# Leaving out 27 idle TensorE products in the norm between the first MLP and the gating unit

## The chip, the cores and the metric

The kernel runs on one core of a Trainium2 chip. A core has TensorE (PE, with its weight loads shown apart as PEld), VectorE (DVE), ScalarE (ACT), GpSimd (POOL) and the sync engine (SP), which issues DMAs. The engines run at the same time and wait for each other through semaphores. The metric is the device time of one execution in microseconds, and lower is better.

## The reference

Two transformer blocks run one after the other on 512 tokens of 1024 channels, in float32. The first block has two layers (a pooling mixer, then a spatial gating unit, "sgu"), each followed by an MLP of width 4096. The second block has attention, a recurrent mixer and a gated feed-forward. The place of the change is the norm that opens the second layer, right behind the first MLP:

```python
for i in range(DEPTH):
    mod = c_act @ ada_w[i] + ada_b[i]
    sh1, sc1, g1, sh2, sc2, g2 = jnp.split(mod, 6, axis=-1)
    h = modulate(rmsnorm(x, norm_mix_g[i]), sh1, sc1)      # i == 1: this norm
    y = pool_mixer(h, ...) if i == 0 else sgu_mixer(h, sgu_w_in, ...)
    x = x + g1[:, None, :] * y
    h = modulate(rmsnorm(x, norm_mlp_g[i]), sh2, sc2)
    x = x + g2[:, None, :] * sq_relu_mlp(h, mlp_w1[i], mlp_w2[i])

def rmsnorm(x, g):
    y = x * lax.rsqrt(jnp.mean(x * x, axis=-1, keepdims=True) + RMS_EPS)
    return y * g
def sgu_mixer(h, w_in, ...):
    z = gelu(h @ w_in)      # the first use of this norm's h
```

## The kernel before

Activations lie transposed: `xT[:, k]` holds 128 channels (k = 0 to 7) by 512 tokens. Weights come in slabs of 512 by 512 through DMAs that SP issues. ACT rounds each slab into its high part (`w_hi`, line 1665) and DVE subtracts to get its low part (`w_lo`, line 2309), in a ring of two slabs. TensorE then makes three products for one (high by high, high by low, low by high), each 128 rows by 512 columns, 48 for a slab; that is the function `slab`, line 762. The activations are split in the same way into `h_hi` and `h_lo`.

Each engine has one program, written out by hand in the order in which it runs, and semaphores alone tie the engines together. There is no scheduler: what stands behind a waiting instruction on an engine waits too.

The norm `NORM_MIX1` goes through these steps. The last slab of `mlp(0, ...)` fills four banks. DVE adds each to `xT` (line 2667) and ACT squares it (line 1683). DVE sums the squares (line 2336). `norm_mean` lets TensorE sum over the channels with 16 products of one column each (line 733, each recorded twice). ACT takes the root (line 1687), DVE the reciprocal (line 2324) and puts it on a diagonal (line 2326). `norm_spread` is one product of 512 columns, recorded as two (line 837), that spreads the diagonal over all partitions in a bank. Then, for k = 0 to 7, DVE scales `xT[:, k]` into `tmp` (line 2346), ACT makes `h_hi[:, k]` (line 1693) and DVE makes `h_lo[:, k]` (line 2356). The first slab of `sgu_in` (`two_slabs("sgu_in", 0, ...)`, with `k_outer=True`) begins as soon as k = 0 is made and does 12 products for each k.

The function `keep_busy(s, times, b=6)` multiplies a slab's `w_hi` with itself `times` times into bank 6 (line 820). Nobody reads what it makes, and the next true use of the bank starts it anew. It stands three times in this norm: 7 products ahead of the mean, 6 between the mean and the spread, and 14 behind the spread. It is used at two later places as well (lines 1236 and 1619), which the change leaves alone.

Three other places of the program come up in the prediction. The norm ahead of the first MLP (`NORM_MLP0`, some 60 to 76 us into the trace) has the same steps with no such products. The gating unit's last heads and its output slab (lines 1044 and 1098, 528 to 537 us) run just behind this part. The norm ahead of the second MLP (596 to 600 us) uses `mlp1_by_halves` and DVE line 2784.

Of the kernel before, what the change touches and what calls it, by code (L numbers as in the profile page):

```python
# [92 lines left out]
SLABS = {"mlp0": 0, "sgu_in": 41, "sgu_out": 49, "mlp1": 53, "proj": 94, "w_out": 104, "ffn": 108}  # L93
# [632 lines left out]
def tensor_program(te, t, m, sem):  # L726
# [88 lines left out]
    def keep_busy(s, times, b=6):  # L815

        w_hi = m.ring(s)[0]
        te.wait_ge(sem("hi_made"), s + 1)
        for _ in range(times):
            te.matmul(bank[:, b], w_hi[:, 0, 0:P], w_hi[:, 0], start=True, stop=True)  # L820

    def norm_mean(norm, squares):

        name, count = added(norm, additions(norm))
        te.wait_ge(sem(name), count)
        apart = norm in LAST_APART
        for j in range(4):
            mm = in_halves(bank[:, 4, j:j + 1], squares[:, 3, P * j:P * j + P], m.mean_ones[:, 0:1], j == 0, not apart)
        if apart:
            te.wait_ge(sem("squared"), 8 * norm + 8)  # L830
            for j in range(4):
                mm = in_halves(bank[:, 4, j:j + 1], squares[:, 0, P * j:P * j + P], m.mean_ones[:, 0:1], False, True)
        mm.then_inc(sem("meaned"), 1)

    def norm_spread(norm):
        te.wait_ge(sem("diag_made"), norm + 1)
        te.matmul(m.rstd_bank, ones[:, :], m.rstd_diag[:, :, :].rearrange("p j t -> p (j t)"),
                  start=True, stop=True).then_inc(sem("spread"), 1)
# [210 lines left out]
    norm_spread(NORM_MLP0)  # L1049
    ada_sums(7)  # L1050
    mlp(0, NORM_MLP0)
    keep_busy(SLABS["sgu_in"], 7)
    norm_mean(NORM_MIX1, m.quartered["mlp0"].squares)
    keep_busy(SLABS["sgu_in"], 6)
    norm_spread(NORM_MIX1)
    keep_busy(SLABS["sgu_in"], 14)


    def two_slabs(name, g, hi, lo, before_k=None, weights_stationary=True, k_outer=False, beside=None):
# [2531 lines left out]
def program(nc, t, out):  # L3591
    m, sem = Places(nc), Sems(nc)
    tensor_program(nc.tensor, t, m, sem)
    scalar_program(nc.scalar, t, m, sem)
    vector_program(nc.vector, t, m, sem)
    gpsimd_program(nc.gpsimd, t, m, sem)
    sync_program(nc.sync, t, out, m, sem)
# [47 lines left out]
```

## Time and profile before

| | us |
|---|---|
| median of 3 runs | 1757.35 (1757.21 to 1757.66) |
| the profiled execution, its own time | 1758.68 |
| its span, first to last instruction | 1757.3 |
| TensorE busy | 1715.4 (98%) |
| DVE busy | 1227.5 (70%) |
| ACT busy | 757.1 (43%) |

Between the span and the profiled execution's own time lie 1.4 us, and that execution took 1.3 us more than the median of the runs. Matmuls are pipelined: a product of 512 columns is shown with some 0.39 us, while the next one starts 0.227 us after it, so the distance between starts is what a product costs in a stream. The granted clock is given as a share: 1.00 is 2.4 GHz and 0.50 is 1.2 GHz.

### The profile page before, as it was taken

To read this page: it belongs to the slowest core of one execution; us is meant where nothing else is said; L and a number is where in the kernel's file an instruction comes from. 1 tells how busy PE (TensorE), PEld (TensorE's weight loads), DVE (VectorE), ACT (ScalarE), POOL (GpSimd) and SP (SyncE) were. 2 spreads that over 40 slices of the span, in tenths; PEclk is the share of its full clock that TensorE was granted. 3 is DMA by queue.
4 is the path that set the end of the run, shared out by engine and by line. 5 is a ranking of instruction groups with operands and counts; after the bars stand their busy time and mean duration, and the time that the engine had idled before them with its cause. 6 is when DMAs were issued, how large, how long until landed. Compare 5 with 4: busy or idle time off the path is not lost. (4 is left out here: it accounts for less than half of the span.)

```text
span 1757.3 us, 23082 instructions
## 1 busy us (share of the span) xinstructions
PE 1715.4 (98%) x9391; PEld 1397.5 (80%) x9391; DVE 1227.5 (70%) x1435; ACT 757.1 (43%) x933; POOL 126.0 (7%) x131
## 2 busy tenths in 40 slices
PE   7899999999999999999999998999999999999997
PEld 4488888888789888888887786778888888888886
DVE  4588797876874675747457777775768579578579
ACT  4354435333332553535345523453544344344344
POOL 0111010000100000000000011110000000000002
PEclk9899999999999999999999999999999999999999
DMA  9967484745632445445221331003344435336324
GB/s 369 409 195 229 129 252 134 260 143 192 216 105 87 145 120 144 144 120 168 96 67 65 103 86 51 5 1 121 120 120 123 141 96 154 126 80 189 99 72 132
DMA packets 141673, 246.45 MB, mean 140 GB/s; under 512 B 15117, under 2 KB 50597, under 8 KB 141312
## 3 DMA queue, kind: packets, MB, share of 16 engines
q1 hardware_dynamic: 122432, 192.76, 32.3%
q0 software_dynamic: 18992, 51.62, 11.9%
q8 instruction: 75, 1.23, 0.3%
q10 hardware_dynamic: 144, 0.59, 0.1%
q14 instruction: 30, 0.25, 0.0%
HBM read 239.69 MB, written 6.83 MB: 140 GB/s over the span
## 5 line engine op out<-in xcount | busy, mean ns | idle before, releaser
L2309 DVE TENSOR_TENSOR w_lo<-raw,w_hi 128x2048 fp32r<-128x2048 f32 x99 | 227.5, 2298 | 160.7 <-ACT w_hi L1665 160.2
L1665 ACT ACTIVATE w_hi<-raw 128x2048 fp32r<-128x2048 f32 x103 | 197.2, 1915 | 275.3 <-PE bank L762 170.4
L762 PE MATMUL bank<-h_hi,w_hi 128*128 128x512 f32 x720 | 285.1, 396 | 6.1 <-DVE h_lo L2356 2.9
L762 PE MATMUL bank<-h_hi,w_lo 128*128 128x512 f32 x720 | 281.0, 390 | 0.0
L762 PE MATMUL bank<-h_lo,w_hi 128*128 128x512 f32 x720 | 280.9, 390 | 0.0
L762 PE MATMUL bank<-f_lo,w_hi 128*128 128x512 f32 x496 | 193.0, 389 | 0.0
L762 PE MATMUL bank<-f_hi,w_hi 128*128 128x512 f32 x496 | 193.0, 389 | 0.0
L762 PE MATMUL bank<-f_hi,w_lo 128*128 128x512 f32 x496 | 193.0, 389 | 0.0
L762 PEld LDWEIGHTS bank<-h_hi,w_hi 128*128 128x128 f32 x720 | 135.6, 188 | 38.0 <-issue 10.5
L762 PEld LDWEIGHTS bank<-h_hi,w_lo 128*128 128x128 f32 x720 | 135.4, 188 | 28.6
L762 PEld LDWEIGHTS bank<-h_lo,w_hi 128*128 128x128 f32 x720 | 135.6, 188 | 27.6 <-issue 0.5
L787 PE MATMUL bank<-w_hi,blocks_hi_mlp 128*128 128x512 f32 x336 | 131.2, 391 | 0.0
L787 PE MATMUL bank<-w_hi,blocks_lo_mlp 128*128 128x512 f32 x336 | 130.8, 389 | 0.0
L787 PE MATMUL bank<-w_lo,blocks_hi_mlp 128*128 128x512 f32 x336 | 130.8, 389 | 0.0
L762 PEld LDWEIGHTS bank<-f_hi,w_lo 128*128 128x128 f32 x496 | 93.1, 188 | 19.5
L762 PEld LDWEIGHTS bank<-f_lo,w_hi 128*128 128x128 f32 x496 | 93.1, 188 | 19.3
L762 PEld LDWEIGHTS bank<-f_hi,w_hi 128*128 128x128 f32 x496 | 93.1, 188 | 19.1
L2309 DVE TENSOR_TENSOR w_lo<-raw_more_ffn,w_hi 128x2048 fp32r<-128x2048 f32 x30 | 68.7, 2290 | 46.7 <-ACT w_hi L1665 46.5
L1665 ACT ACTIVATE w_hi<-raw_more_ffn 128x2048 fp32r<-128x2048 f32 x30 | 57.5, 1916 | 77.8 <-PE bank L787 37.2
L787 PE MATMUL bank<-w_hi,blocks_hi_ffn 128*128 128x512 f32 x224 | 87.3, 390 | 0.6 <-issue 0.6
L787 PE MATMUL bank<-w_hi,blocks_lo_ffn 128*128 128x512 f32 x224 | 87.2, 389 | 0.0
L787 PE MATMUL bank<-w_lo,blocks_hi_ffn 128*128 128x512 f32 x224 | 87.2, 389 | 0.0
(486 smaller groups left out, 3138.2 us busy)
## 6 DMA issues: line engine op xcount, KB each, us to landing
raw<-in_mlp_w SPq DMA_DIRECT2D x82, 512.0 KB, 5.1
ada_ring<-in_ada_w SPq DMA_DIRECT2D x12, 2048.0 KB, 15.1
ada_ring<-in_ada_w POOLq DMA_DIRECT2D x16, 1024.0 KB, 7.3
raw_more_mlp<-in_mlp_w SPq DMA_DIRECT2D x32, 512.0 KB, 4.8
raw<-in_w_ffn_up SPq DMA_DIRECT2D x32, 512.0 KB, 5.0
raw_more_ffn<-in_w_ffn_up SPq DMA_DIRECT2D x32, 512.0 KB, 4.9
xT<-in_mlp_w SPq DMA_DIRECT2D x26, 512.0 KB, 4.8
raw<-in_w_in SPq DMA_DIRECT2D x20, 512.0 KB, 4.5
```

Source lines behind the costliest of these rows:

```text
L762: mm = te.matmul(bank[:, b + n], x, y, start=first and k == 0 and j == 0, stop=last and k == 3 and j == 2, skip_group_check=s in (SLABS["m ...
L787: mm = te.matmul(bank[:, b + n], x, w[:, k], start=start and k == 0 and j == 0, stop=k == 3 and j == 2, skip_group_check=True)
L1665: se.activation(m.ring(s)[0], m.raw_place(s), ACT.Copy).then_inc(sem("hi_made"), 1)
L2309: ve.tensor_tensor(lo, m.raw_place(s), hi.bitcast(F32), ALU.subtract).then_inc(sem("lo_made"), 1)
```

## The change

Three calls are taken out of TensorE's program, 7 + 6 + 14 = 27 products. Nothing else is edited.

```diff
     mlp(0, NORM_MLP0)
-    keep_busy(SLABS["sgu_in"], 7)
     norm_mean(NORM_MIX1, m.quartered["mlp0"].squares)
-    keep_busy(SLABS["sgu_in"], 6)
     norm_spread(NORM_MIX1)
-    keep_busy(SLABS["sgu_in"], 14)
```

Each call also had a wait on `hi_made` for the first slab of `sgu_in`; that slab's own products wait for the same count. On TensorE the stretch between the last slab of the first MLP and the first products on `sgu_in` then reads as follows, as a difference of the two programs.

```order
 L762 MATMUL bank<-blocks_lo_mlp,w_hi 128x512
 L762 MATMUL bank<-blocks_hi_mlp,w_lo 128x512
-L820 MATMUL bank<-w_hi 128x512 x7
 L733 MATMUL bank<-mean_ones,quarter_u_mlp 64x1 x16
-L820 MATMUL bank<-w_hi 128x512 x6
 L837 MATMUL bank<-rstd_diag,ones 128x512
-L820 MATMUL bank<-w_hi 128x512 x14
 L762 MATMUL bank<-w_hi,h_hi 128x512
 L762 MATMUL bank<-w_lo,h_hi 128x512
```

No instruction has moved past another. ACT, DVE, POOL and SP keep their instructions and their order.

## Rows read from the trace of the kernel before

**Rows 1.** The page: span, busy time by engine

```profile
span 1757.3 us, 23082 instructions
PE 1715.4 (98%) x9391; PEld 1397.5 (80%) x9391; DVE 1227.5 (70%) x1435; ACT 757.1 (43%) x933; POOL 126.0 (7%) x131
```

**Rows 2.** Waits of TensorE behind 433 us: total, times, longest

```profile
PE bank L762 <- DVE h_lo L2784: 2.9, 1, 2.9
PE bank L1468 <- DVE pt L3173: 2.8, 7, 0.8
```

**Rows 3.** Timeline of the norm, TensorE: start, duration, line, operation, [idle before]

```profile
424.86 1.75 PE L820 MATMUL bank<-w_hi 128*128 128x512 f32 x7
...
427.57 1.66 PE L820 MATMUL bank<-w_hi 128*128 128x512 f32 x6
429.07 1.07 PE L837 MATMUL bank<-rstd_diag,ones 128*128 128x512 f32 x2
...
429.58 3.78 PE L820 MATMUL bank<-w_hi 128*128 128x512 f32 x14
433.20 0.39 PE L762 MATMUL bank<-w_hi,h_hi 128*128 128x512 f32 x1
...
440.90 0.39 PE L762 MATMUL bank<-w_lo,h_hi 128*128 128x512 f32 x1
```

**Rows 4.** Timeline of the same stretch, weight load, DVE and ACT

```profile
426.54 1.01 PEld L733 LDWEIGHTS bank<-mean_ones,quarter_u_mlp 128*64 128x64 f32 x32 [0.35 <-DVE quarter_u_mlp L2336]
...
428.27 0.69 DVE L2326 TENSOR_TENSOR rstd_diag<-const,rstd_rows 128x512 f32<-128x512 f32 x1
429.01 0.30 PEld L837 LDWEIGHTS bank<-rstd_diag,ones 128*128 128x128 f32 x2 [0.22 <-DVE rstd_diag L2326]
...
430.18 1.41 DVE L2346 SCALAR_TENSOR_TENSOR tmp<-xT,gain,bank 128x512 f32<-128x512 f32 x2 [1.22 <-PE bank L837]
...
431.85 0.76 DVE L2356 SCALAR_TENSOR_TENSOR h_lo<-tmp,mod,h_hi 128x512 fp32r<-128x512 f32 x1 [0.26 <-ACT h_hi L1693]
433.37 0.75 DVE L2356 SCALAR_TENSOR_TENSOR h_lo<-tmp,mod,h_hi 128x512 fp32r<-128x512 f32 x1
...
440.30 0.75 DVE L2356 SCALAR_TENSOR_TENSOR h_lo<-tmp,mod,h_hi 128x512 fp32r<-128x512 f32 x1 [0.20 <-ACT h_hi L1693]
```

**Rows 5.** Timeline of the first norm, without idle products, TensorE

```profile
59.45 1.10 PE L733 MATMUL bank<-mean_ones,pooled 128*64 128x1 f32 x32
...
64.07 3.63 PE L881 MATMUL bank<-ada_ring,c_wide 128*32 128x512 f32 x14
67.63 1.70 PE L837 MATMUL bank<-rstd_diag,ones 128*128 128x512 f32 x2
69.27 0.63 PE L733 MATMUL bank<-ones,ada_ring 128*64 128x1 f32 x16
72.84 0.77 PE L762 MATMUL bank<-h_hi,w_hi 128*128 128x512 f32 x1 [2.94 <-DVE h_lo L2356]
...
75.54 0.46 PE L762 MATMUL bank<-h_hi,w_hi 128*128 128x512 f32 x1
```

**Rows 6.** Windows, TensorE: stretch, length, busy (count), granted clock, DMA share, GB/s

```profile
61.50:62.00 0.50, 0.10 (x4) 1.00 1.04 406
...
62.00:69.00 7.00, 6.73 (x48) 0.51 1.05 404
...
72.25:72.75 0.50, 0.00 (x0) 0.50 1.04 406
...
530.00:533.00 3.00, 3.00 (x28) 1.00 0.02 5
...
533.00:537.00 4.00, 4.00 (x17) 0.57 0.00 0
```

**Rows 7.** Timeline, TensorE, the modulation sums ahead of the gating heads (as rows 3)

```profile
528.68 3.63 PE L1044 MATMUL bank<-ones,late_acc 128*128 128x1 f32 x32
```

**Rows 8.** Window over the gap ahead of the second MLP, columns as in rows 6

```profile
596.40:599.30 2.90, 0.00 (x1) 1.00 0.37 66
```

## The prediction

> **What bounds the kernel now.** I read the page first: TensorE is busy for 1715.4 of 1757.3 us [rows 1]. Then its waits: behind the place of the change they are few and short, the longest 2.9 us, and each is for DVE or ACT work that starts from a product of TensorE itself [rows 2]. So from the first MLP on there is no reserve that would swallow a delay: what TensorE loses or gains near 425 us should arrive at the end nearly in full. Third comes the timeline of the norm, once for TensorE [rows 3] and once for the engines it waits for [rows 4]. What the reader is to look for there is which of the three groups of idle products ends later than the thing that TensorE would otherwise wait for. Last come the places where TensorE is thinly used and no idle products stand: what the granted clock did there and what that cost [rows 5 to 8].
>
> **The 7 products ahead of the mean: nothing in time.** They start at 424.86 and cost 0.227 us each in a stream (the 34 steps from the product at 433.20 to the one at 440.90 take 7.70 us) [rows 3], so their last one has been fed in by 426.45. The weight load of the mean starts at 426.54, behind 0.35 us of idleness that ended with DVE's last addition of squares [rows 4]. Without the seven the wait is longer, and the mean starts at the same time.
>
> **The 6 ahead of the spread: nothing either.** They start at 427.57 and are fed in by 428.93 [rows 3]. The diagonal is ready at 428.27 + 0.69 = 428.96, and the spread's weight load starts at 429.01 with 0.22 us of idleness ahead of it [rows 4].
>
> **The 14 behind the spread: a small gain.** Here the group ends later than what it covers. The first `h_lo` is ready at 431.85 + 0.76 = 432.61 [rows 4], but the first true product starts only at 433.20, directly behind the fourteen [rows 3]. The spread shows how long TensorE takes where only a wait stands in between: its first record starts 0.11 us behind the diagonal [rows 3, 4]. With as much behind `h_lo` the product could start at 432.72, a gain of 0.48 us. The next pieces are in time for that: k = 1 is ready at 434.12, and twelve products later TensorE wants it at 435.44; k = 4 is ready at 441.05 and is wanted, after 48 products, at 443.6 [rows 4]. DVE, not TensorE, sets the start of k = 0 only.
>
> **What the idle products cover: the granted clock.** Without them TensorE is thinly used from 425.1, where the last true product of the MLP is fed in, to 432.7, which is some 7.6 us. Inside lie only the 16 one-column products of the mean and the spread's 1.07 us. The first norm of this same kernel has such a stretch. Dense work ends there at 59.45, one-column products follow, and at 62.0 the granted clock falls from 1.00 to 0.50 (2.4 to 1.2 GHz), for nearly seven microseconds [rows 5, 6]. A second fall has come by 72.25, some 3 us after the one-column products that began at 69.27; a third comes just behind 533.0, over 4.3 us after one-column products began at 528.68 [rows 5 to 7]. So the clock fell 2.5 to 4.4 us after dense work gave way to thin work. Counted from 425.1, that puts the fall between 427.6 and 429.5, behind the mean and before or in the spread.
>
> *The spread at the lower clock.* The same two records take 1.70 us at 67.63, where the clock was 0.50, against 1.07 us here [rows 3, 5]. All that follows hangs on it (DVE's `tmp` started 0.04 us after the spread's end). Cost: +0.63 us, or nothing if the clock still stands; I take 0.63, since three falls out of three would come before the spread is over.
>
> *The restart at the lower clock.* The products on `sgu_in` then start slow. In rows 5 the first slab of the first MLP starts at 72.84 right after a fall, and its seventh product starts at 75.54: 2.70 us for six steps that cost 6 x 0.227 = 1.36 us at the full clock. That is a loss of 1.34 us, half of the time spent at the lower level, and it is the lower bound: same line, same form, same kind of gap. The upper bound is the first fall, where dense products of 512 columns ran from 64.07 on and the clock came back only at 68.9 (0.51 over 62.0 to 69.0), 4.8 us later [rows 5, 6]; half of that is 2.4 us. Between the two I take the middle, 1.9 us. The stretch ahead of this restart is thin for longer (7.6 us) than the 2.94 us in rows 5, which speaks against the lower end, but the rows that reach the upper end used 32 of the 128 columns of the array, which speaks against that one.
>
> **The sum.** 0.63 - 0.48 + 1.9 = +2.05 us on the path of TensorE. Against the profiled execution's own 1758.7 us it would be 1760.8; that execution lies 1.3 us above the median of the runs for a reason the trace doesn't show, so I put the sum on the median: 1757.35 + 2.05 = 1759.4. With the bounds of the two clock terms it goes from 1757.35 + 0 - 0.48 + 1.34 = 1758.2 to 1757.35 + 0.63 - 0.48 + 2.4 = 1759.9.
>
> In rows 5 six products ran wholly at the lower clock before it rose. The Trainium skill, page "TensorE: Matmul & The Clock Gate", section on what is actually happening in the clock gate, says that the number of cold products differs between runs of one and the same kernel and names 6, 11 and 14 for one kernel. By it the restart would be an estimated 1.2 to 2.8 us (0.2 us for each product) in place of 1.3 to 2.4, and the sum by the page +1.4 to +3.0; the trace has one execution and can't show the spread between runs. The same page, in its table of what matters for a kernel, warns against idle gaps of around 3 us between bursts, which speaks against this change; the trace agrees in the falls of rows 6 and disagrees in rows 8.
>
> **Rivals.** *The clock does not fall, and the idle products only stood in the way.* For it speaks the gap ahead of the second MLP: TensorE is empty from 596.4 to 599.3, the clock stays at 1.00 [rows 8]. Against it: that gap is 2.9 us between two dense stretches, while here 7.6 us are thin. It would give 1757.35 - 0.48 = 1756.9. This is also the case in which the change does not bring what its removal of 27 products suggests: 27 x 0.227 = 6.1 us of TensorE's time go, and only 0.48 of it lay on the path.
>
> *One fall brings another: slower.* The gap at 596.4 did not lower the clock in this trace, and the one of the same length at 69.9 did [rows 5, 6, 8]. What the clock does is thus decided by where such a gap lies, not by its length alone, and a delay of about 2 us moves that gap. If it now falls as well, the first slab of the second MLP restarts slow for another 1.9 us: 0.63 - 0.48 + 1.9 + 1.9 = +3.95, 1761.3, and with 2.4 for each +4.95, 1762.3. The place is the line of products that waits for `h_lo` of line 2784, and the case crosses +3.5 us once the two restarts together cost over 3.4 us. Against it: the fall at 533.0 could by the same shift be avoided, which would give back some 1.7 us (half of the 3.4 us that 0.57 over 533.0 to 537.0 means).
>
> *DVE instead of TensorE becomes the bound in the first slab.* A restart at the lower clock makes TensorE ask later for each k, so `h_lo` is in time all the more. I give it no chance of its own.
>
> **How the numbers follow.** A difference of 0.2%, 3.5 us, is about what a measurement can tell from no change. The clock falls and the cost stays in place: 0.65, 1759.4. The clock doesn't fall: 0.17, 1756.9. A second fall: 0.14, 1761.3, nearly all of it beyond 3.5 us. The remaining 0.04 is for later falls that go away or come on. All of the first two cases are within 0.2%. So slower 0.15, same 0.83, faster 0.02. The range holds both bounds of the first case, reaches down to the second and takes in a part of the third: 1756.8 to 1761.2.
>
> **What the profile afterwards would show.** The mean should start at the same distance behind DVE's last addition, and the spread behind the diagonal: if either starts earlier, the 7 or the 6 were on the path. The granted clock should be 0.50 in a window that begins between some 2.5 and 4.4 us behind the MLP's last product and ends some 3 to 5 us behind the first product on `sgu_in`; the spread's two records should take about 1.7 us. The first true product should start some 0.11 us behind the first `h_lo`, and the twelve products for k = 0 should take over 4 us in place of 2.7. At 596 to 600 us the gap should be as long as before. Wrong would be the prediction if the clock stays at 1.00 throughout, if it stays low far beyond 4.8 us of dense work, or if the stretch ends later as forecast and the end of the program does not.

## The result

The kernel after takes 1764.03 us (median of 7 executions, 1760.64 to 1768.61), the kernel before 1757.70 us (7 executions, 1757.21 to 1760.25). The ratio is 1.0033, with a 95% interval of 1.0023 to 1.0042: slower by about a third of a per cent. The forecast was 1759.4 us with a range up to 1761.2 and "no measurable change" as the likeliest case; the time lies above the range.

The page of the kernel after, its span and its busy time by engine. The lines answer to [rows 1].

```profile
span 1762.7 us, 23028 instructions
PE 1715.6 (97%) x9364; PEld 1397.1 (79%) x9364; DVE 1227.4 (70%) x1435; ACT 757.3 (43%) x933; POOL 126.1 (7%) x131
```

TensorE has 27 products fewer and is busy as long as before: the same work runs more slowly. The timeline of TensorE in the stretch of the change (start, duration, line, operation, idle time before it and what ended it) answers to [rows 3]:

```profile
423.93 0.39 PE L762 MATMUL bank<-blocks_hi_mlp,w_lo 128*128 128x512 f32 x1
425.76 1.24 PE L733 MATMUL bank<-mean_ones,quarter_u_mlp 128*64 128x1 f32 x32 [1.44 <-DVE quarter_u_mlp L2333]
428.37 2.08 PE L837 MATMUL bank<-rstd_diag,ones 128*128 128x512 f32 x2 [1.37 <-DVE rstd_diag L2323]
433.05 0.77 PE L762 MATMUL bank<-w_hi,h_hi 128*128 128x512 f32 x1 [2.60 <-DVE h_lo L2353]
...
436.60 0.49 PE L762 MATMUL bank<-w_hi,h_lo 128*128 128x512 f32 x1
```

Each wait that an idle product covered now shows as idle time: 1.44, 1.37 and 2.60 us. The mean starts 0.05 us behind DVE's last addition (0.13 before). The spread takes 2.08 us in place of 1.07, and eight products run at nearly double distance before the ninth, at 436.60, sees the clock rise. The windows of TensorE there (stretch, length, busy time with count, granted clock, DMA share, GB/s) show what they had in common:

```profile
424.00:426.00 2.00, 0.56 (x10) 1.00 0.00 0
426.00:428.00 2.00, 1.01 (x30) 0.64 0.81 236
428.00:433.00 5.00, 2.08 (x2) 0.50 1.01 387
433.00:436.50 3.50, 3.45 (x8) 0.50 0.99 322
436.50:438.50 2.00, 2.00 (x9) 0.92 0.92 316
```

The clock was low for 10.2 us, from 2.2 us behind the end of the MLP's last product to 3.75 us behind the start of the first true product. Two later places were at the full clock in the trace before and are not in this one, 471 and 604 us. Windows of the kernel after, same columns:

```profile
466.00:470.00 4.00, 4.00 (x20) 1.00 0.69 237
470.00:475.00 5.00, 5.00 (x15) 0.66 0.70 261
535.00:540.00 5.00, 5.00 (x27) 0.66 0.01 3
603.00:608.00 5.00, 5.00 (x17) 0.66 0.48 147
```

A mean of 0.66 over 5 us means 3.4 us at the lower clock. The one at 536 us is the one of [rows 6] at 533. What stands ahead of the fall at 471 us is thin work, not idleness: eight transposes of the gating weights and four records of products on a single row. In the timeline TensorE is busy without a break:

```profile
467.55 1.03 PE L1077 MATMUL bank<-const,ws 128*128 128x128 f32 x8
468.52 1.98 PE L1080 MATMUL bank<-bs_row,ones 1*128 1x512 f32 x4
470.43 0.50 PE L762 MATMUL bank<-w_hi,h_hi 128*128 128x512 f32 x1
...
471.05 0.63 PE L762 MATMUL bank<-w_hi,h_lo 128*128 128x512 f32 x1
```

Ahead of 604 us stands the wait of 2.9 us of [rows 8]. It is as long as before, and this time the clock falls behind it:

```profile
602.59 0.47 PE L762 MATMUL bank<-h_hi,w_hi 128*128 128x512 f32 x1 [2.93 <-DVE h_lo L2781]
```

So the difference of the two spans, 5.4 us, can be laid out by the starts of products that both timelines have:

| stretch | before | after | difference |
|---|---|---|---|
| start to the MLP's last product | 424.64 | 423.93 | -0.71 |
| from there to the first transpose of the gating weights (the norm and its first two slabs) | 41.20 | 43.62 | +2.42 |
| from there to the sums of the gating weights at 478 us (the fall at 471 us lies in it) | 8.49 | 10.05 | +1.56 |
| from there to the second MLP's first product | 109.15 | 109.17 | +0.02 |
| from there to its 151st product of `h_hi` by `w_hi` at 634 us (the fall at 604 us lies in it) | 45.16 | 46.80 | +1.64 |
| from there to the end | 1128.66 | 1129.16 | +0.50 |

The first row is the first norm, which the change does not touch: the clock was low there for 6.8 us in place of 10.2. The stretch of the change itself accounts for 2.4 us. The question for the experiments is what the other 3 us are: part of the change, or chance.

### The profile page after: what moved, and what is told of

It reads as the page before. It is cut to its first block and busy times, and to the rows that moved or that the text cites. A ratio compares the mean times of both kernels' runs of the same rounds, so it can differ in the third digit from the quotient of the medians.

```text
span 1762.7 us, 23028 instructions
## 1 busy us (share of the span) xinstructions
PE 1715.6 (97%) x9364; PEld 1397.1 (79%) x9364; DVE 1227.4 (70%) x1435; ACT 757.3 (43%) x933; POOL 126.1 (7%) x131
## 5 line engine op out<-in xcount | busy, mean ns | idle before, releaser
L762 PEld LDWEIGHTS bank<-h_hi,w_hi 128*128 128x128 f32 x720 | 135.9, 189 | 38.2 <-issue 10.5
```

Source lines behind the costliest of these rows:

```text
L762: mm = te.matmul(bank[:, b + n], x, y, start=first and k == 0 and j == 0, stop=last and k == 3 and j == 2, skip_group_check=s in (SLABS["m ...
```

## The experiments

In the tables a mean is over all executions of a kernel, and its error is the standard deviation over the root of their number. "Before" is the kernel before on the same chip in the same job.

**The kernel before once more.**

> The kernel before, unchanged, to see how its granted clock and its time differ between executions. Theory A (in place): the change costs the 2.4 us that the traces show at 425 to 437 us, and the falls of the clock at 471, 536 and 604 us that only the trace after has are matters of chance that this kernel has as often. Then its executions spread as those after the change do (some 8 us between lowest and highest), its clocks lie between 0.985 and 0.993, and the second trace of it has falls at other places than the first. Theory B (one fall brings others): they belong to the change. Then this kernel stays at 1757 to 1758 us, clock 0.993, with the same falls as in the first trace.

| | executions | mean | lowest to highest |
|---|---|---|---|
| before, beside it | 35 | 1759.50 +- 0.38 | 1756.36 to 1764.45 |
| before again | 12 | 1759.32 +- 0.48 | 1756.90 to 1761.70 |

The kernel before is not at 1757.4: its executions spread over 8 us, like those after the change. Over the 35, time follows the time at the lower clock (1 less the mean granted clock, doubled, times the span): 1750.0 us + 0.37 for each such us, with a scatter of 0.8 us left. That is between what the change's own spell costs for each low us (2.4 us for 10.2, since a part of it lies over waits) and what the spells at 471 and 604 us cost over dense products (1.56 and 1.64 us for 3.4). And the second trace of it has the fall at 471 us that the first had not, and none at 604:

```profile
424.00:438.00 14.00, 14.00 (x88) 1.00 0.71 257
...
470.50:475.00 4.50, 4.50 (x14) 0.62 0.65 233
599.00:608.00 9.00, 6.07 (x28) 1.00 0.47 127
```

Theory A is right in that later falls come and go with no edit at all. Whether they come as often remained to be seen.

**A delay without a fall.** In the kernel before, behind the spread:

```diff
-    keep_busy(SLABS["sgu_in"], 14)
+    keep_busy(SLABS["sgu_in"], 25)
```

> The kernel before with 25 idle products behind the spread in place of 14. The clock stays up at 425 to 437 us, and all that follows starts 11 x 0.227 = 2.5 us later, as much as the change delays it. Theory A: +2.5 us over before and no more. Theory B in the form that the delay moves the later thin places to where they lower the clock: +2.5 us and 1.5 to 4 us on top, with falls at about 471, 536 or 604 us. If it gives +2.5 us without them, the later falls hang on the first fall or on chance, not on the delay.

Mean 1761.35 +- 0.42 (12 executions) against 1759.50 +- 0.38: +1.9 +- 0.6, ratio 1.0009 (1.0000 to 1.0019), at 26.4 us low against 25.7. In the trace the first true product starts 11.03 us behind the MLP's last product in place of 8.56, so the 2.5 us are there; the mean adds nothing on top, and the time at the lower clock did not grow. A delay of this size alone did not bring more falls. This trace has the fall at 604 us (windows of this kernel), and none at 471:

```profile
468.00:476.00 8.00, 8.00 (x32) 1.00 0.51 187
598.00:607.00 9.00, 7.41 (x26) 0.81 0.57 151
```

**Each group by itself.** First the 14 taken out and the 7 and 6 kept, then the other way round:

```diff
-    keep_busy(SLABS["sgu_in"], 14)
```

> The kernel before without the 14 idle products behind the spread, the 7 and the 6 kept. The thin stretch is then the spread (1.07 us of full products) and the wait of 2.6 us for the first h_lo, like the gap of 2.9 us ahead of the second MLP, which did not lower the clock in the first trace and did in the trace after. Theory A: the spread stays at 1.07 us, the first true product starts 0.48 us earlier, and the clock falls in some executions only: -0.5 to +1.4 us, median near +0.5. Theory B: the same when it does not fall, and +3 to +6 us when it does.

```diff
-    keep_busy(SLABS["sgu_in"], 7)
...
-    keep_busy(SLABS["sgu_in"], 6)
```

> The kernel before without the 7 and the 6, the 14 behind the spread kept. Thin from 425.1 to 429.9 us with the spread inside. If the clock falls at 427.6 to 429.5 us, the spread takes up to 1.7 us in place of 1.07 us, and the 14 themselves run at the lower clock, 0.427 us each, until it rises. Theory A: 0 to +3.5 us, median +2. Theory B: +3 to +8 us, as the change.

| | executions | mean | ratio to before (95%) | us low |
|---|---|---|---|---|
| only 7 and 6 | 12 | 1760.64 +- 0.67 | 1.0007 (0.9995 to 1.0019) | 30.2 |
| only 14 | 12 | 1761.46 +- 0.72 | 1.0011 (0.9999 to 1.0022) | 31.1 |

Without the 14 the traced execution kept its clock in the stretch. The timeline of TensorE and the windows of that kernel:

```profile
427.71 1.07 PE L837 MATMUL bank<-rstd_diag,ones 128*128 128x512 f32 x2
431.38 0.47 PE L762 MATMUL bank<-w_hi,h_hi 128*128 128x512 f32 x1 [2.60 <-DVE h_lo L2355]
...
424.00:431.30 7.30, 4.78 (x46) 1.00 0.77 277
431.40:437.00 5.60, 5.60 (x25) 1.00 1.00 341
```

From the spread's start to the first true product it is 3.67 us here and 4.13 in [rows 3]: the 14 did hold the product up, by 0.46 us, as the prediction had it (0.48). With the 14 alone the clock falls before they start. In that kernel's timeline they fill 5.92 us and hold up the first true product:

```profile
428.91 2.07 PE L837 MATMUL bank<-rstd_diag,ones 128*128 128x512 f32 x2 [1.37 <-DVE rstd_diag L2324]
429.99 5.92 PE L820 MATMUL bank<-w_hi 128*128 128x512 f32 x14
435.76 0.39 PE L762 MATMUL bank<-w_hi,h_hi 128*128 128x512 f32 x1
```

From the spread's start to the first true product it is 6.85 us, where the kernel after needs 4.68 with a spread as slow. The whole stretch from the MLP's last product to the first transpose is 43.8 us, as dear as without any idle product (43.62), although the spell is shorter (6.8 us). In the means the two kernels lie 1.1 +- 0.8 and 2.0 +- 0.8 us over the kernel before. The first is not clear of noise; its traced execution escaped the fall, but its 4.5 us more at the lower clock in the mean suggest that others did not. The second is still some 2.7 +- 1.0 us below what the change costs in the mean (4.65, next experiment), so one trace is not the rule for all its executions.

**The change once more.**

> The kernel after, unchanged, beside the kernel before on one chip. So far time follows the time that the granted clock stood low: before = 1750.0 + 0.37 for each us at the lower clock, over 35 executions with 26 us low on average; after = 1748.7 + 0.36 for each, over 7 executions with 43 us low. Theory A (the stretch at 425 to 437 us alone, 7 to 10 us low and +2.0 to +3.3 us; later falls are chance in both kernels): after lies 2 to 3.5 us over before, with 33 to 36 us low on average, and the +6.4 us of the first comparison (7 executions on each side) was luck with the later falls. Theory B (one fall brings others, or the change makes them likelier): again +5.5 to +7 us and over 40 us low.

Mean 1763.21 +- 0.80 (12) against 1758.76 +- 0.35 (31): +4.5 +- 0.9, ratio 1.0027 (1.0016 to 1.0038), 38.2 us low against 25.3. That is between the two theories. Over all jobs the kernel before has a mean of 1759.10 +- 0.16 (156 executions) and the kernel after 1763.75 +- 0.58 (20): +4.65 +- 0.6 us. The first comparison had 1758.18 and 1764.55, so it was lucky for the kernel before by some 0.9 us and unlucky for the other by 0.8. The trace of this run has all three spells, of 10.2, 3.4 and 3.4 us (windows):

```profile
424.00:438.00 14.00, 8.59 (x50) 0.63 0.80 288
470.00:476.00 6.00, 6.00 (x18) 0.72 0.68 256
603.00:609.00 6.00, 5.81 (x19) 0.72 0.49 161
```

**The later gaps covered, with and without the change.** Twelve idle products in the wait at 596 us, and the transposes one tile earlier, so that a tile of dense products lies between them and the products on one row:

```diff
+                    if layer and q + g == 0:
+                        keep_busy(s + k, 12)
                     slab(s + k, group, m.h_hi[:, 4 * k:4 * k + 4], ...)
...
-        if (k, n) == (0, 3):
+        if (k, n) == (0, 2):
             ...
             mm.then_inc(sem("ws_turned"), 1)
+        elif (k, n) == (0, 3):
             for q in range(2):
```

> The kernel before with two later thin places taken away: 12 idle products in the wait of 2.9 us ahead of the second slab of the second MLP (596 us), and the eight transposes at 466 us moved one tile of products ahead of the four products on one row that followed them. Theory A: the falls at 471 and 604 us, which came in three and in three of six traces, are gone, each worth 3.4 us low and some 1.3 to 1.6 us; the mean falls by 1 to 2 us, the low time from 26 to about 22 us, and the executions spread less. If these places don't cause the falls, nothing changes.

> The kernel after, with the same two places taken away. The difference to the run with the idle products (later gaps covered in both) is the change without what it could bring about at 471 and 604 us. Theory A: +2 to +3.5 us over that run, the same as without the covers. Theory B: the difference shrinks from about 6 to about 3 us because the covered places were where the rest came from.

| | executions | mean | ratio to before (95%) | us low |
|---|---|---|---|---|
| before, gaps covered | 11 | 1758.38 +- 0.43 | 0.9997 (0.9987 to 1.0007) | 24.9 |
| after, gaps covered | 7 | 1763.71 +- 0.77 | 1.0027 (1.0015 to 1.0039) | 39.8 |

The cover at 596 us worked, the split at 466 us didn't: both traces still fall, at 469 and 472 us. The windows of the first of the two, and its timeline:

```profile
464.00:475.00 11.00, 11.00 (x38) 0.84 0.54 196
598.00:607.00 9.00, 8.82 (x39) 1.00 0.53 136
```

```profile
466.29 1.98 PE L1086 MATMUL bank<-bs_row,ones 1*128 1x512 f32 x4
...
469.29 0.63 PE L762 MATMUL bank<-w_lo,h_hi 128*128 128x512 f32 x1
```

Dense products ran for 2.9 us between the transposes and these records (463.4 to 466.3), and the clock fell at 469.2. So the 1.98 us on one row stood ahead of a fall by themselves.

The difference, +5.3 +- 0.9, did not shrink as theory B wanted, but only the place at 596 us was taken away.

**The first norm filled.** Two and three idle products between the parts of the mean, and eleven behind the spread, in a free bank:

```diff
             mm = in_halves(bank[:, 4, j:j + 1], m.pooled[:, 2 * p, ...], ...)
+        if p in (1, 2):
+            keep_busy(SLABS["mlp0"], p + 1, 3)
...
     norm_spread(NORM_MLP0)
     ada_sums(7)
+    keep_busy(SLABS["mlp0"], 11, 3)
```

> The kernel before with idle products in the first norm as well: 2 and 3 between the parts of its mean, 11 in the wait of 2.94 us ahead of the first MLP. If the lower clock costs there what it costs at 425 us: the falls at 62 and 72 us go or shrink, 3 to 10 us less at the lower clock, and -1 to -3 us. Against: TensorE waits for loads there with the DMA engines full, and eleven products at the lower clock take 4.7 us in a wait of 2.9 us, so where the clock is down already they delay the slab by 1.8 us. I expect -1 us.

Mean 1757.61 +- 0.40 (11) against 1758.76 +- 0.35: -1.15 +- 0.5, ratio 0.9993 (0.9984 to 1.0001), 20.4 us low against 25.3. The falls of [rows 5, 6] at 62 and 72 us are gone; the window 60 to 76 us of this kernel has the clock at 1.00:

```profile
60.00:76.00 16.00, 15.80 (x138) 1.00 1.05 407
```

In exchange this trace has a spell of 3.4 us at 112 us, which no other of the 20 traces has.

**Does the delay decide where the clock falls?** Idle products behind the norm's first two slabs, where TensorE is dense, move all that follows:

```diff
+    keep_busy(SLABS["sgu_in"] + 2, 4)      # or 8
     two_slabs("sgu_in", 1, m.h_hi, m.h_lo, weights_stationary=False, beside=spatial_weights)
```

> The kernel after, plus 4 idle products behind the first two slabs of the gating unit, where TensorE is dense anyway: they only move everything behind them by 0.9 us. Alignment theory (the change puts the thin places at 468 and 602 us to where they lower the clock; each fall costs 1.6 us): both falls go in the usual execution, so 0.9 - 1.6 - 1.6 = -2.3 us against the kernel after, near +2 us over before. Chance theory (later falls come as often whatever the delay): +0.9 us against after, +5.4 over before.

> The same with 8 idle products, 1.8 us. Alignment theory: the fall at 471 us goes, the one at 604 us comes again: 1.8 - 1.6 = +0.2 us against after, near +4.7 over before. Chance theory: +1.8 against after, +6.3 over before.

> The kernel before with the same 8 idle products in the same place. Alignment theory: the fall at 471 us comes in the usual execution where before it did not: 1.8 + 1.6 = +3.4 us over before. Chance theory: +1.8 us over before.

| | executions | mean | against its own kernel | alignment wanted | chance wanted |
|---|---|---|---|---|---|
| after + 4 | 11 | 1762.74 +- 0.60 | -0.5 +- 1.0 | -2.3 | +0.9 |
| after + 8 | 11 | 1763.54 +- 0.48 | +0.3 +- 0.9 | +0.2 | +1.8 |
| before + 8 | 11 | 1760.68 +- 0.45 | +1.8 +- 0.5 | +3.4 | +1.8 |

"Its own kernel" is, for the kernel after, its twelve executions under "The change once more", and for the kernel before the 32 beside these runs. At 471 and 604 us the three traces did what alignment said. After + 4 has neither of the two falls, after + 8 only the one at 605 us, before + 8 the one at 471 us. After + 4 also had a shorter spell in the change's own stretch, 6.8 us, and one at 991 us that no other trace has. Windows of after + 4, then of before + 8:

```profile
469.00:475.00 6.00, 6.00 (x26) 1.00 0.49 175
602.00:608.00 6.00, 6.00 (x28) 1.00 0.51 83
```

```profile
469.00:476.00 7.00, 7.00 (x23) 0.76 0.48 170
```

The means are divided. Before + 8 costs what the products themselves cost and lies 1.6 us (error 0.5) below what alignment wanted. After + 4 lies between the two, 1.4 us below chance (error 1.0), and after + 8 is where alignment put it, 1.5 us below chance (error 0.9). Whether a shift of one or two microseconds decides a fall is not shown, since falls come and go between executions of one kernel as well.

After + 8 and before + 8 are also a pair that differs by the change alone: +2.9 +- 0.7 us and 10.0 us more at the lower clock, what its own stretch costs and little more.

**Idle products where the clock falls.** The first norm filled, 12 in the wait at 596 us, and 12 in place of 14 behind the spread.

> The kernel before with idle products where they pay: the first norm as in the run with it filled (2, 3 and 11), 12 in the wait of 2.9 us ahead of the second slab of the second MLP, and 12 in place of 14 behind the spread, so that the first true product is not held up. From the parts: about -1.1 us for the first norm (measured -1.15 with an error of 0.5), -0.45 for the two products, -0.5 for the gap (1.6 us in a third of the executions): -2 us against before.

Mean 1756.72 +- 0.50 (11) against 1758.86 +- 0.31 (32): -2.1 +- 0.6, median 1755.99 against 1758.78, ratio 0.9987 (0.9978 to 0.9996), 18.8 us low against 26.1. It is faster than both kernels, though its trace has a longer spell than the kernel before at the gating heads (529 to 536 us, 6.8 us in place of 3.4). The eleven products in the first norm leave a wait of 0.20 us only and the first slab starts at the full clock. Its timeline of TensorE answers to [rows 5]:

```profile
65.17 1.13 PE L837 MATMUL bank<-rstd_diag,ones 128*128 128x512 f32 x2
...
66.79 2.82 PE L820 MATMUL bank<-w_hi 128*128 128x512 f32 x11
69.80 0.47 PE L762 MATMUL bank<-h_hi,w_hi 128*128 128x512 f32 x1 [0.20 <-DVE h_lo L2361]
```

**Both later places covered in earnest, with and without the change.** The wait at 596 us as above, and the thin work at 466 us cut into four pieces between tiles of dense products:

```diff
+        if k == 0 and n < 2:      # four transposes each
+            for hh in range(4 * n, 4 * n + 4):
+                mm = te.transpose(bank[:, 4 + hh // 4, ...], m.ws[:, hh], ident)
+        elif k == 0:              # one bias product each
+            q = n - 2
+            mm = te.matmul(bank[:, 6 + q], ones[0:1, :], m.bs_row[0:1, ...], start=True, stop=True)
```

> The kernel before, with the thin work at 466 us cut into four pieces of 0.5 to 1 us that lie between tiles of dense products (four transposes, four transposes, one bias product, one bias product), and 12 idle products in the wait at 596 us. The falls at 471 and 604 us should be gone, which moving the transposes alone did not do (it left 2 us of thin work in one piece and a fall at 469 us). Each is worth 1.6 us where it comes. Expected: -0.5 to -1.3 us against before.

> The kernel after with the same. The change is worth 2.4 us in its own stretch (three traces of it), and +4.5 to +4.7 us over before in the means. Theory 'more falls later': the 2 us over are falls at 471 and 604 us that come more often behind the change, so that against the covered kernel before it is only +2.4 to +3 us. If it stays at +4.5, the rest lies elsewhere (533, 1062 us, or the stretch itself costs more in the executions without a trace).

| | executions | mean | ratio to before (95%) | us low |
|---|---|---|---|---|
| before, both covered | 11 | 1757.28 +- 0.35 | 0.9991 (0.9982 to 0.9999) | 20.8 |
| after, both covered | 6 | 1763.37 +- 0.95 | 1.0024 (1.0009 to 1.0039) | 38.8 |

The covers work in both traces (clock 1.00 at 471 and at 604 us) and that kernel lies 1.8 +- 0.6 us below the kernel before. But the difference between the two is +6.1 +- 1.0, and theory "more falls later" wanted 2.4 to 3. In the trace with the change the own stretch costs more than before, 36.17 us from the MLP's last product to the first transpose against 33.05 (+3.1), because the clock fell later (3.9 us behind the MLP's last product) and so stayed low for 5.6 us of dense products in place of 3.75. The fall at 533 us is longer too, 6.8 us against 3.4. Its windows:

```profile
424.00:440.00 16.00, 10.59 (x55) 0.68 0.73 264
469.00:478.00 9.00, 9.00 (x37) 1.00 0.61 223
533.00:542.00 9.00, 9.00 (x46) 0.62 0.01 2
603.00:610.00 7.00, 6.82 (x31) 1.00 0.54 160
```

Two further traces, of the unchanged kernels:

> The kernel before once more, for its trace: which of the falls at 471, 604 and 1062 us it has. So far, of four traces with the clock up at 425 to 437 us and nothing moved behind it, two have the fall at 471 us and one that at 604 us. Chance theory: any of them. Theory 'more falls later': at most one of the two.

> The kernel after once more, for its trace. Own stretch: 10.2 us low and +2.4 us from the MLP's last product to the transposes at 468 us, as in the two traces so far. Theory 'more falls later': both 471 and 604 us again. Chance theory: any of them.

Their windows at 471 and 604 us, first the kernel before, then the kernel after:

```profile
468.00:474.00 6.00, 6.00 (x20) 0.72 0.54 193
597.00:606.00 9.00, 6.08 (x29) 1.00 0.42 122
```

```profile
469.00:475.00 6.00, 6.00 (x19) 0.72 0.58 214
602.00:608.00 6.00, 6.00 (x21) 0.72 0.50 137
```

Three traces of each kernel thus give:

| | own stretch, us | fall at 471 | fall at 604 | fall at 1062 |
|---|---|---|---|---|
| before | 41.20, 41.18, 41.19 | 2 of 3 | 0 of 3 | 3 of 3 |
| after | 43.62, 43.62, 43.60 | 3 of 3 | 3 of 3 | 2 of 3 |

**All thin places of the first 620 us out of the way but the change's own.** The pair once more, with the first norm filled as well.

> The kernel before with all of it: first norm filled, 471 and 604 us covered, 12 idle products in place of 14 behind the spread. From the parts: -1.15 for the first norm, -1.8 for the covered places, -0.45 for two products: about -3 us against before, 1755.7 to 1756.5, and no more than 16 us at the lower clock.

> The same without the 7, the 6 and the 12, so this pair is the change once more, with the other thin places of the first 620 us out of the way. Own stretch alone: 10.2 us or less more at the lower clock and +2.0 to +3.5 us over its partner (0.45 us of that for the two products fewer in the partner). If the difference is again +5 us or more with 15 us or more at the lower clock, falls at 533 and 1062 us add to it, and the trace should show them longer than in its partner.

| | executions | mean | ratio to before (95%) | us low |
|---|---|---|---|---|
| all filled | 11 | 1757.17 +- 0.42 | 0.9992 (0.9982 to 1.0002) | 17.6 |
| all but the change's 27 | 12 | 1760.95 +- 0.53 | 1.0007 (0.9998 to 1.0017) | 28.5 |

The difference is +3.8 +- 0.7 us and 10.9 us at the lower clock, no more than one spell of 10.2. The own stretch is as large: 36.20 us from the MLP's last product to the first transpose against 32.67, +3.5, of which 0.45 because the partner has 12 and not 14 products behind the spread. The two traces differ in more than that: besides the own spell the one without the 27 has 6.8 us at 533 us against 3.4, and spells at 1066 and 1189 us that its partner lacks (1763.75 and 1753.49 us). The means say that such extras are not the rule in this pair. Its windows show nothing at 471 and 604 us:

```profile
424.00:438.00 14.00, 9.37 (x50) 0.63 0.85 300
469.00:476.00 7.00, 7.00 (x29) 1.00 0.59 220
532.00:541.00 9.00, 9.00 (x45) 0.62 0.01 2
597.00:607.00 10.00, 9.82 (x56) 1.00 0.31 112
```

By itself the first half of this pair lies 2.3 +- 0.6 us below the kernel before (the interval of its ratio just passes 1), no better than the simpler version above.

## Why the prediction was wrong

**The 7 and the 6 cost nothing in time: right.** Mean and spread start 0.05 us behind DVE in place of 0.13 and 0.11, with 1.44 and 1.37 us of open wait, and from the MLP's last product to the spread it is 4.44 us in place of 4.43.

**The 14 hold the first product up by 0.48 us: right.** Measured 0.46, in the run without them at the full clock.

**The clock falls: right, a little early.** It fell 2.2 us behind the end of the MLP's last product where 2.5 to 4.4 was forecast. The 425.1 from which the forecast counts was 0.2 us too late: the first idle product starts at 424.86 [rows 3].

**The spread at the lower clock, +0.63 us: too small.** It took 2.08 us, +1.01. The 1.70 us of [rows 5] was a mixed row: the clock rose at 68.9, and it ran from 67.63 to 69.33. A duration next to a change of clock is no price for either level, and the windows of [rows 6] showed as much.

**The restart, +1.9 us: right.** From the first true product to the first transpose 34.50 us in place of 32.65, +1.85, half of the 3.75 us for which the clock was low there.

So the own stretch was forecast at +2.05 and measured at +2.4 in the three traces of the kernel after. Where other things were altered too it was 1.55 once (after + 4, less its four products), 2.4 twice and 3.1 twice (less the 0.45 of the last pair). The spell was 10.2 us long in seven of these eight traces, but it began 2.2 to 4.2 us behind the MLP's last product, and the later it began, the more dense products it covered: 3.7 to 6.1 us of them, and the restart cost 1.85 to 2.9 us, half of that.

**"The clock falls and the cost stays in place": the step that failed.** The sum has no term for falls behind the own stretch, and the likeliest case (0.65) put them at nothing. In the means the change costs 4.65 +- 0.6 us where its own stretch costs 2.4, and it brings 14.1 +- 1.5 us at the lower clock where its own spell has 10.2. So some 2.2 us and some 4 us of low time came on top. All three traces of the kernel after have the falls at 471 and 604 us, 1.56 and 1.64 us in the one laid out above; of the three of the kernel before two have the first and none the second. The rival "one fall brings another" had named the gap at 596 us and priced it at 1.9 us, with a chance of 0.14. And it had overlooked 471 us, because I looked for idle gaps in the list of waits and this place has none: TensorE is busy there with transposes and products on one row. In [rows 7] such thin work ahead of the fall at 533 us was in plain sight.

**The base: failed too.** I set the sum on 1757.35, the median of three executions within 0.45 us of each other, and passed over the profiled one at 1758.68. The mean of 156 executions is 1759.1. The three had luck, by the fit above some 20 us at the lower clock in place of 26 (an estimate, no clock of theirs is on record). From 1759.1 the same sum would have been 1761.2. Of the 4.6 us between 1759.4 and the measured 1764.03 the base is thus 1.75, the own stretch 0.35, what came on top 2.25 and the luck of the seven executions 0.3. In the comparison itself the kernel before had a median of 1757.70, so there the base was nearly right and the luck of the two sides larger.

**What stays open.** Five pairs differ by the change alone:

| pair | difference, us | more us low | own stretch in the traces |
|---|---|---|---|
| before and after, all executions | +4.65 +- 0.6 | 14.1 +- 1.5 | +2.4 |
| wait at 596 us covered in both | +5.3 +- 0.9 | 14.9 +- 2.1 | +2.4 |
| 8 idle products later in both | +2.9 +- 0.7 | 10.0 +- 1.6 | +2.4 |
| 471 and 604 us covered in both | +6.1 +- 1.0 | 18.0 +- 3.1 | +3.1 |
| first norm filled as well | +3.8 +- 0.7 | 10.9 +- 1.6 | +3.5 |

In the third and the fifth the own stretch is nearly the whole cost; in the others 2 to 3 us and 4 to 8 us of low time come on top. That the change makes the falls at 471 and 604 us more frequent fits the traces of the first pair (six against two), but six traces are few, and the fourth pair, which has neither fall in its traces, speaks against these two places as the whole of it. The longer spell at 533 us, in two traces of the eight without the 27 products and in one of the twelve with a group of them, is a candidate that no run took away. Where the rest comes from, and how much of it is the luck of few executions, was not settled.

## What to carry to other kernels

A stretch in which TensorE is thinly used costs half of every dense microsecond until the clock is back. Idle products belong ahead of the fall: where it came first, the 14 alone took 5.92 us in place of 3.78 and gave nothing back in the stretch. Look for such stretches in the granted clock by windows, not in the list of waits, and take a duration as a price only where the clock stood still. When a kernel's time follows its time at the lower clock, three executions that agree prove little: compare the sum of low time, and many executions on both sides.

## What the runs showed of the hardware that was not expected

The executions of one and the same kernel lie up to 9 us apart (1755.15 to 1764.45 for the kernel before), and 0.3 to 0.4 us of time for each microsecond at the lower clock explains them to within 0.6 to 1.0 us. A place at which the clock falls in one execution leaves it alone in the next: the wait of 2.9 us at 596 us lowered it in all three traces of the kernel after and in none of three before, and over all kernels that left it open in 6 of 13 traces. With 12 idle products in it there was no fall in 7 traces.

Full occupation is no protection. Eight transposes and four one-row records, 2.9 us in which TensorE is never idle, stood ahead of a fall in 8 of 14 traces. In the two traces with the transposes moved away the clock fell behind the one-row records alone, 1.98 us, and in the four in which all of it was cut into pieces of 0.6 to 1.1 us between dense tiles it did not fall. The Trainium skill, page "TensorE: Matmul & The Clock Gate", part 4 on the transpose through TensorE, says that transposes don't count as busy in the same way; no run here shows what they do by themselves. The Trainium skill, same page, in its table of what matters for a kernel, advises against idle gaps of more than about 3 us; the falls at 471 us came without an idle gap.
